# A hybrid decoder block on one core: another table of early visits, and another order of ACT's and DVE's small work around the turnings

## The reference

```
ada = c @ w_ada + b_ada;  shift, scale, gate = split(ada, 3)
h    = rms_norm(x, g_pre) * (1 + scale) + shift
proj = h @ w_in            # q, c_kv, k_rope, q_diff, k_diff, v_diff, gates, merge gates
A = MLA(proj) * silu(gate_mla) @ w_o_mla
B = DiffAttn(proj) * silu(gate_diff) @ w_o_diff
y = (sigmoid(mg_mla) * A + sigmoid(mg_diff) * B) @ w_out
out = x + gate * rms_norm(y, g_post)
```

## Time and profile before

| | us |
|---|---|
| median of 3 runs (lowest, highest) | 766.32 (766.23, 766.82) |
| the profiled execution | 766.46 |
| its span, first to last instruction | 764.6 |
| PE busy | 753.5 |
| DVE busy | 562.6 |
| ACT busy | 418.3 |

### The profile page before, as it was taken

How to read it: one execution, slowest core, us unless ns; L and a number is a source line. 1 busy time by engine, 2 the same in 40 slices (tenths; PEclk the granted TensorE clock), 3 DMA queues, 4 the chain that set the end, 5 groups by cost and what they waited for, 6 DMA issues and landing times.

```text
span 764.6 us, 10078 instructions
## 1 busy us (share of the span) xinstructions
PE 753.5 (99%) x3681; PEld 624.5 (82%) x3681; DVE 562.6 (74%) x823; ACT 418.3 (55%) x612; POOL 21.5 (3%) x94
## 2 busy tenths in 40 slices
PE   7999999999999999999999999999999999999997
PEld 5877788888888988888888888888888888888885
DVE  4899999889868579888887768776554556465554
ACT  5678777665567554544545564655444444444441
POOL 2000000000000000000000000011100000000000
PEclk9999999999999999999999999999999999999999
DMA  9999999999674789888887575555666666567642
GB/s 339 395 392 395 390 392 342 359 352 293 199 213 130 212 279 295 296 278 283 286 294 194 162 214 181 167 170 165 183 176 195 193 182 199 189 206 251 219 155 110
DMA packets 132555, 189.71 MB, mean 248 GB/s; under 512 B 10325, under 2 KB 68122, under 8 KB 132250
## 3 DMA queue, kind: packets, MB, share of 16 engines
q1 hardware_dynamic: 132240, 188.77, 75.2%
q10 hardware_dynamic: 266, 0.30, 0.1%
HBM read 185.90 MB, written 2.10 MB: 246 GB/s over the span
## 4 chain that ended last, share of the span: by engine, by line
PE 90%; DMA 3%; SPq 2%; issue 2%; ACT 2%; DVE 2%; DVEq 0%; POOLq 0%; POOL 0%; ACTq 0%
PE ps L1895 17%; PE ps L1897 17%; PE ps L1896 17%; PE ps L1885 13%; PE ps L1854 8%; PE ps L1871 6%; PE ps L1857 4%; DMA w_raw<-in_w_in 3%; SPq L523 2%; PE ps L1690 1%; ACT w_both L1022 1%; DVE ada_acc L1298 1%; PE ps L1675 1%; PE ps L1705 1%; PE ps L1848 1%
## 5 line engine op out<-in xcount | busy, mean ns | idle before, releaser
L1546 DVE TENSOR_TENSOR w_both<-w_raw,w_both 128x1024 fp32r<-128x1024 f32 x248 | 301.8, 1223 | 158.1 <-ACT w_both L1022 156.9
L1022 ACT CAST w_both<-w_raw 128x1024 fp32r<-128x1024 f32 x248 | 259.2, 1050 | 244.6 <-PE ps L1897 184.2
L1885 PE MATMUL ps<-w_both,h_both 128*128 128x512 f32 x560 | 138.7, 390 | 0.0
L1885 PEld LDWEIGHTS ps<-w_both,h_both 128*128 128x128 f32 x560 | 105.0, 188 | 22.6 <-DVE w_both L1546 0.4
L1895 PE MATMUL ps<-w_both,h_both 128*128 128x512 f32 x296 | 116.9, 395 | 0.0
L1897 PE MATMUL ps<-w_both,h_both 128*128 128x512 f32 x296 | 115.4, 390 | 0.0
L1896 PE MATMUL ps<-w_both,h_both 128*128 128x512 f32 x296 | 115.2, 389 | 0.0
L1871 PE MATMUL ps<-w_both,h_both 128*128 128x512 f32 x280 | 76.1, 394 | 0.8 <-ACT h_both L978 0.7
L1298 DVE SCALAR_TENSOR_TENSOR ada_acc<-ada_ring,cols,ada_acc 128x512 f32<-128x512 f32 x98 | 69.7, 746 | 0.5
L1895 PEld LDWEIGHTS ps<-w_both,h_both 128*128 128x128 f32 x296 | 55.6, 188 | 12.7 <-issue 1.7
L1897 PEld LDWEIGHTS ps<-w_both,h_both 128*128 128x128 f32 x296 | 55.5, 188 | 11.7
(11 more groups left out here) (261 smaller groups left out, 844.0 us busy)
## 6 DMA issues: line engine op xcount, KB each, us to landing
w_raw<-in_w_in SPq DMA_DIRECT2D x177, 512.0 KB, 4.6
ada_ring<-in_w_ada SPq DMA_DIRECT2D x128, 256.0 KB, 6.6
gate_ring<-in_w_ada SPq DMA_DIRECT2D x32, 512.0 KB, 5.6
w_raw<-in_w_out SPq DMA_DIRECT2D x32, 512.0 KB, 3.6
w_raw<-in_w_o_mla SPq DMA_DIRECT2D x16, 512.0 KB, 3.9
w_raw<-in_w_o_diff SPq DMA_DIRECT2D x16, 512.0 KB, 4.1
w_raw<-in_w_ukv SPq DMA_DIRECT2D x16, 256.0 KB, 3.5
x_tok<-in_x SPq DMA_DIRECT2D x2, 1024.0 KB, 6.0
```

The source lines that it names most:

```text
L1022: act.copy(w_hi[:, p % RING, :], w_raw[:, p % RING, :]).then_inc(hi_done, 1)
L1546: dve.tensor_tensor(w_lo[:, p % RING, :], w_raw[:, p % RING, :], w_hi[:, p % RING, :].bitcast(F32), ALU.subtract).then_inc(lo_done, 1)
L1885: ins = mm(ps[:, b0 + t, :], lhsT=side[:, 2 * i + r, t * P:(t + 1) * P], rhs=w[:, p % RING, r * CH:(r + 1) * CH], start=False, stop=last a ...
```

## The change

The table `PERIODS` is another one: 30 visits in 69 pieces instead of 31 in 70. Some visits run on over a turning. The turnings stand before pieces 8, 16, 24, 33, 43, 53 and 62, so the second period has 8 pieces and the fourth 9. The first uses of the pairs are pieces 10, 18, 26, 35, 45, 55 and 64, always the third piece of a period. 16 visits are seeded and 6 add. The four gate groups come in another order behind the stage.

ACT's sum of every turning now hangs on the turning's own piece, its `make_h` on the next and its `make_full` on the one behind that. In ACT's loop the sum stands ahead of `make_h`. Copies (`act_early`) before the second turning come one piece sooner, and a seed whose bank is emptied on the same piece comes behind that copy, others before. The join of DVE stands in a function of its own: for turning 1 it comes behind the seventh part instead of in the eighth, for the others it comes before the wait for the eighth load instead of after it.

```
-    [(("ckv", 0), (0, 1)), 0, (("vd", 0), (1,)), (("vd", 1), (1,)), 1, TURN, (("gate", 3), (1,)), (("gate", 0), (1,))],
+    [(("ckv", 0), (0, 1)), (("vd", 0), (1,)), 0, (("vd", 1), (1,)), (("q", 2), (1,)), 1, TURN, (("gate", 0), (1,)), (("gate", 1), (1, 2))],
...
-SEEDED = [8, 9, 10, 12, 13, 14, 15, 16, 17, 19, 20, 21, 22, 23, 24]
+SEEDED = [v for v in range(8, 25) if v != 12]
...
-        sum_after = {place + (j > 1): j for place, j in sum_before.items()}
-        h_after = {place + 1: j for place, j in sum_after.items()}
-        full_after = {place + 2: j for place, j in sum_after.items()}
+        sum_after = {place: j for place, j in sum_before.items()}
+        h_after = {place + 1: j for place, j in sum_before.items()}
+        full_after = {place + 2: j for place, j in sum_before.items()}
...
-        seed_at[SEEDED[0]] += 1
...
+        drained_at = {v: visit_end[v] + (1 if visit_end[v] < turn_at[2] and visit_end[v] not in sum_after else 2)
+                      for v in COPIED}
+        for v in SEEDED:
+            if drained_at.get(v - 2, seed_at[v]) < seed_at[v]:
+                act_after[seed_at[v]].append(act_seed(v))
         for v in COPIED:
-            act_after[visit_end[v] + (1 if visit_end[v] < turn_at[1] else 2)].append(act_early(v))
+            act_after[drained_at[v]].append(act_early(v))
         for v in SEEDED:
-            act_after[seed_at[v]].append(act_seed(v))
+            if drained_at.get(v - 2, seed_at[v]) == seed_at[v]:
+                act_after[seed_at[v]].append(act_seed(v))
...
+                if p in sum_after:
+                    sum_mod(sum_after[p])
                 if p in h_after:
                     make_h(h_after[p])
                 if p == 0:
                     make_first_h()
-                if p in sum_after:
-                    sum_mod(sum_after[p])
...
+            def join(j):
+                n = (j + 1) * (KT // 2) - 1
+                acc = acc_of_group(j)
+                eng.wait_ge(ada_odd, n)
+                eng.wait_ge(ada_used, n)
+                dve.tensor_tensor(acc[:, 0, :], acc[:, 0, :], acc[:, 1, :], ALU.add).then_inc(ada_joined, 1)
...
+                if joined and j > 1:
+                    join(j)
...
+                    if (j, q) == (1, KT // 2 - 2):
+                        join(1)
```

More of the change, by code:

```diff
@@ L83, in make_jobs @@
 def make_jobs():
-    jobs = [("kr", 0), ("gate", 1), ("vd", 0), ("gate", 2), ("vd", 1), ("gate", 3)]
+    jobs = [("kr", 0), ("gate", 3), ("vd", 0), ("gate", 1), ("vd", 1), ("gate", 2)]
     for n in range(2):
@@ L102 @@
      (("gate", 2), (0,)), (("gate", 3), (0,)), 1, TURN, (("q", 2), (0,))],
-    [(("ckv", 0), (0, 1)), 0, (("vd", 0), (1,)), (("vd", 1), (1,)), 1, TURN, (("gate", 3), (1,)), (("gate", 0), (1,))],
[L104 to L109, removed]
+    [(("ckv", 0), (0, 1)), (("vd", 0), (1,)), 0, (("vd", 1), (1,)), (("q", 2), (1,)), 1, TURN, (("gate", 0), (1,)), (("gate", 1), (1, 2))],
+    [0, (("gate", 2), (1, 2)), (("gate", 0), (2,)), 1, TURN, (("gate", 3), (1, 2, 3))],
+    [0, (("vd", 0), (2, 3)), (("vd", 1), (2, 3)), 1, TURN, (("q", 2), (2, 3, 4))],
+    [0, (("ckv", 0), (2, 3, 4)), (("gate", 0), (3, 4)), 1, TURN, (("gate", 1), (3, 4, 5))],
+    [0, (("gate", 2), (3, 4, 5)), (("vd", 0), (4, 5)), 1, TURN, (("vd", 1), (4, 5, 6))],
+    [0, (("q", 2), (5, 6)), (("gate", 0), (5, 6)), 1, TURN, (("ckv", 0), (5, 6, 7))],
+    [0, (("q", 2), (7,)), 1, (("gate", 0), (7,))],
 ]
@@ L1388, in ada_part @@
                     eng.wait_ge(ada_turned, j - 1)
-                eng.wait_ge(ada_in[n % ADA_RING], 32 * (n // ADA_RING + 1))
                 acc = acc_of_group(j)
                 joined = q == KT // 2 - 1
+                if joined and j > 1:
+                    join(j)
                 if joined:
-                    eng.wait_ge(ada_odd, n)
-                    eng.wait_ge(ada_used, n)
-                    dve.tensor_tensor(acc[:, 0, :], acc[:, 0, :], acc[:, 1, :], ALU.add).then_inc(ada_joined, 1)
                     eng.wait_ge(ada_joined, j)
+                eng.wait_ge(ada_in[n % ADA_RING], 32 * (n // ADA_RING + 1))
                 for t, done in ((1, ada_odd), (0, ada_used)):
```

## The result

The changed kernel takes 775.05 us (774.99 to 775.79, 4 runs) against 766.51 of the kernel before: a ratio of 1.0113 with an interval of 1.0101 to 1.0125. The direction of the forecast was right. The size, 8.5 us in place of 1.4, was not, and lies outside the range.

A forecast was written before the change was run, and what follows sets the result against it. PE was taken to bound the input stage. Losses of 0.08 by turning 3, 0.31 at it and 1.20 at turnings 4 to 7 sum to 1.59 us more, forecast 767.9 us, range 766.4 to 768.8.

The forecast's parts named there:

- What bounds the kernel: Input stage: PE bounds it; whatever PE loses or is spared there reaches the kernel's end one for one.
- Part 1: Turning 1: the join ahead of piece 7's low part brings it from 44.80 to 44.60, gain 0.20 us.
- Part 2: Turnings 2 to 7: sum ahead of next cast loses 0.31 us at turning 3, 0.30 each at 4-7.
- Part 3 and 4: Periods between turnings 1 and 3: ACT, then DVE late; turning 2 at 67.80, turning 3 at 91.44, 0.08 us later.
- Part 5: Later periods, one visit less, gate groups: nothing beyond the sums' waits; gate groups bounded by 0.3 either way.
- A: Turnings 2 and 3: copies and DVE keep up, only waits behind the sums remain; 766.2 us, chance 0.20 with mixtures.
- B: Whole stage: the sums cost nothing either, turning 3 comes 2.24 us sooner; 764.1 us, chance 0.05.
- C: Third period 0.3 us longer by DVE's add, opening pieces' low parts late 0.1 each; 768.8 us, chance 0.13.
- D: Pieces behind waits: PE starts again for free, 0.10 less behind turnings 3 to 7; 767.2 us, chance 0.04.

The follow-up runs named there:

- a5: Changed kernel with DVE's add of visit 26 alone hung on piece 61 in place of 62: 772.08 us, ratio 1.0069 to the kernel before.
- a2: Changed kernel with ACT's sum at every turning hung behind the cast of the next piece: 772.44 us, ratio 1.0074 to the kernel before.
- b1: Kernel before with the four angle steps on DVE two pieces sooner (pieces 59 to 62): 768.39 us, ratio 1.0022.
- a1: Changed kernel with the four angle steps on DVE two pieces later: 771.50 us, ratio 1.0062 to the kernel before.
- d1: Changed kernel with angle steps three pieces later, visit 26's add on piece 61, sums behind next cast, every join behind seventh part: 766.32 us, 0.9996.
- b2: Kernel before with ACT's sum at turnings 2 to 7 on the turning's own piece, make_h and full value one piece sooner: 775.85 us, 1.0116.

## Where the prediction was right, and the step that failed

**What bounds the kernel**: right. Every wait of PE in the stage went to the end one for one: 8.52 us at the stage's end, 8.54 in the medians.

**Part 1**, turning 1 at 44.60: the join did go ahead. Measured 44.89 in the changed kernel, where ACT waited 0.56 and 0.48 us for the loads of pieces 2 and 3, and PE had lost 0.26 by piece 7; 44.60 in a5. Right within what the loads vary.

**Part 2**, 0.30 at each later turning: right in mechanism, shown by a2, and a little small. The turnings drift by 0.34 to 0.36 (table above). In the rows of turning 4 PE starts the piece behind the wait 0.05 after the end of its cast (120.41 to 120.46), not 0.15; this piece takes 2.87 (120.46 to 123.33) in place of my 2.82, so the third piece is at T + 6.18, and the opening piece takes another 0.10 more (123.33 to 126.15); this is the low part with 0.02 us to spare, which I had seen and left at nothing. The piece behind the wait is slower than its 2.72 by 0.15. Its weight load (PEld) starts at the same moment as its first matmul, released by the cast:

```profile
120.46 0.76 PEld L1885 LDWEIGHTS ps<-w_both,h_both 128*128 128x128 f32 x4 [0.36 <-ACT w_both L1027]
```

The Trainium skill, "TensorE: Matmul & The Clock Gate", section "Architectural detail: the array is 16× 32×32, not 1× 128×128", lets PE's queue pull weight loads ahead of matmuls in flight. Behind a wait for a cast the trace shows no load pulled ahead, and the restart was not free.

**Part 3 and 4**, turning 2 at 67.80 and turning 3 at 91.44: measured 68.14 and 91.78, each 0.34 late, 0.29 of it from turning 1. The period between them was 23.64, as worked out (23.64). That DVE is late last at turning 3 is in the row (0.39 behind DVE's line 1303). This part held, and so did the saying that the gain of the table would be given back by ACT's and DVE's order.

**Part 5** is the step that failed: "The later periods ...: nothing beyond part 2." I had looked at how many ada parts fall on a piece, not at what else hangs on the numbers near the stage's end. The angle steps are tied to `PH1`, turning 7 and visit 26 to the table; they moved in opposite directions, by two pieces against each other. The order of DVE's queue in the changed kernel showed it: add of visit 25, two low parts and three angle steps ahead of the add of visit 26. In the rows of the changed kernel the sum closes: the last ada part ends some 3.3 us ahead of where PE would turn (195.2 against 198.54), and 7.1 us of other work (195.19 to 202.30) and the add of 1.2 stand behind it, which makes 5.0 of the 5.1 lost. I took it that DVE would be ahead far enough, since it had been before. But at the piece behind whose low part the last ada part stands its lead over PE had shrunk from 3.77 us (piece 59, 184.79 to 188.56) to 1.22 (piece 60, 191.88 to 193.10). A part of it is part 2 itself: it was priced at PE alone, but DVE too waits for the cast behind each sum and starts again from nothing.

```profile
120.44 1.23 DVE L1558 TENSOR_TENSOR w_both<-w_raw,w_both 128x1024 fp32r<-128x1024 f32 x1 [3.48 <-ACT w_both L1027]
```

This is the low part of piece 34, behind turning 4: DVE stood still for 3.48 us and began 0.02 ahead of PE. At turning 7 this is worth 0.95 us, by a2. More of it, by b1 and a2, is in part 5: "9 or 10 pieces for 8 parts" passed over that the period ahead of turning 7 went from 10 pieces to 9, so that PE is there 2.7 us sooner and DVE is not. The missed terms are 5.1 us of wait and, behind it, 1.1 to 1.3 us of half clock.

**Rivals**: A and B did not happen. C had the right direction, and one half of it came true: the low parts of opening pieces came about 0.1 late (the 2.82 of piece 35). The other half, a longer third period, did not, and the large loss lay elsewhere. D is contradicted by the 2.87 just named. No rival held the late add.

## What to carry to other kernels

When a plan's length changes, list all work whose place is counted from its end or from a fixed number, and set it against the work whose place moves with the plan: an engine that takes its list in order will put one ahead of the other without a line being touched. Hiding is a matter of lead: before writing that an engine has idle time for a step, take its distance ahead of the waiting engine at that place, in the changed order, and subtract everything in its queue up to the instruction that is waited for. A period that gets shorter for one engine need not get shorter for another: work both out from the same start. And a long wait of TensorE can cost more than itself: the 3.66 us here brought 1.1 to 1.3 us of half clock, the 2.38 us of a1 none.

## What the runs showed of the hardware that was not expected

The half clock behind one idle stretch: granted 0.50 from 203.6 to 206.3 us behind 3.66 us of wait, with 1.01 us of another wait just ahead, 1.1 to 1.3 us of time. It came again in a2 (0.50 from 201.2 to 203.9, again behind 3.66). Behind 2.38 us of wait (a1) and 1.49 (a5) there was none.

Kernels that are the same up to piece 0 start it at different times in their profiles: 22.69 us before, 22.41 in d1, 23.79 in a2 and 23.88 in b2. In the two late ones PE's granted clock was low in the first 20 us. Windows of b2:

```profile
10.00:15.00 5.00, 5.00 (x32) 5.00 (x32) 4.18 (x8) 2.11 (x5) 2.07 (x4) 0.66 1.09 384
```

There the same 64 small matmuls took 9.01 us in place of 7.38. Why some fall into it is open. So a comparison of stages should count from piece 0. By that the stage of a2 is 3.99 us shorter than that of the changed kernel, where the medians differ by 2.6; whether all executions of a2 had the late start is not known.
